# Expert blocks of 64 token slots in place of 96, with room for 23 further blocks, and the down bias added ahead of the expert loop

## The reference, cut to what matters

```python
logits = (h @ w_router + b_router).astype(jnp.float32)
top_val, top_idx = lax.top_k(logits, TOP_K)            # 4 of 32
gate = jax.nn.softmax(top_val, axis=-1)
...
def expert_block(args):
    tok, e = args
    gu = h[tok] @ w_gate_up[e] + b_gate_up[e]
    return clamped_swiglu(gu) @ w_down[e] + b_down[e]
...
y = y * slot_w[:, None].astype(y.dtype)
return jnp.zeros_like(h).at[slot_tok].add(y)
```

## Time and profile before

| what | value |
|---|---|
| median of three runs | 1408.8 us |
| the profiled execution, whole | 1410.75 us |
| its span, first to last instruction | 1408.9 us |
| around the span | 1.85 us |
| granted TensorE clock over the span | 0.959 of full speed |
| TensorE busy | 1294.7 us, 92% of the span |
| moved by DMA | 497.97 MB, mean 353 GB/s |

### The profile page before, as it was taken

How to read it: one execution, slowest core, us unless ns; L and a number is a source line. 1 busy time by engine, 2 the same in 40 slices (tenths; PEclk the granted TensorE clock), 3 DMA queues, 4 the chain that set the end, 5 groups by cost and what they waited for, 6 DMA issues and landing times.

```text
span 1408.9 us, 40022 instructions
## 1 busy us (share of the span) xinstructions
PE 1294.7 (92%) x17444; PEld 820.4 (58%) x17444; DVE 474.1 (34%) x917; ACT 260.2 (18%) x552; POOL 202.1 (14%) x279
## 2 busy tenths in 40 slices
PE   4898999972999999999999999999999999999980
PEld 1796666851566666556666666556666666566640
DVE  0112555655222323322322323322323323322326
ACT  1123444122111111111111111111111111111102
POOL 2205220711100000011000000011000000011003
PEclk9898999985999999999999999999999999999995
DMA  9955586216999999999999999999999999999916
GB/s 332 380 180 173 185 276 213 72 60 253 350 422 423 423 422 423 423 422 423 422 423 423 422 423 420 422 422 422 423 422 423 423 419 422 423 422 423 418 43 223
DMA packets 91214, 497.97 MB, mean 353 GB/s; under 512 B 11972, under 2 KB 15060, under 8 KB 41184
## 3 DMA queue, kind: packets, MB, share of 16 engines
q1 hardware_dynamic: 69552, 437.98, 76.0%
q0 software_dynamic: 13232, 38.78, 7.7%
q10 hardware_dynamic: 8400, 20.82, 4.0%
HBM read 475.20 MB, written 23.25 MB: 354 GB/s over the span
## 4 chain that ended last, share of the span: by engine, by line
PE 72%; DMA 2%; DVE 1%; issue 1%; POOL 0%; ACT 0%; DVEq 0%; ACTq 0%; POOLq 0%
PE ps L1752 47%; PE ps L1765 16%; PE ps L1770 7%; DMA h_rows<-h_parts 2%; PE ps L1739 1%; DVE y_got L1352 1%; PE ps L1720 0%; DMA y_got<-y_rows,y_row_idx 0%; DVE y_got L1357 0%; DMA y_rows<-y_blk 0%; DMA x_slots<-h_rows,slot_tok 0%; POOL y_got L654 0%; DVE x L1364 0%; DVE x L1358 0%; POOL x_slots L640 0%
## 5 line engine op out<-in xcount | busy, mean ns | idle before, releaser
L1752 PE MATMUL ps<-ring,xT 128*32 128x256 f32 x9216 | 511.0, 380 | 9.0 <-DVE xT L1291 9.0
L1752 PEld LDWEIGHTS ps<-ring,xT 128*32 128x32 f32 x9216 | 346.1, 110 | 176.1 <-issue 12.2
L1765 PE MATMUL ps<-y_got,aT 128*32 128x512 f32 x2048 | 279.3, 593 | 0.0
L1305 DVE TENSOR_TENSOR raw<-ps,bias_row 128x768 f32<-128x768 f32 x64 | 61.3, 958 | 474.2 <-PE ps L1752 474.2
L1752 PE MATMUL ps<-y_got,xT 128*32 128x256 f32 x3072 | 176.9, 379 | 0.0
L1770 PE MATMUL ps<-y_got,aT 128*32 128x512 f32 x1024 | 168.6, 592 | 0.0
L1765 PEld LDWEIGHTS ps<-y_got,aT 128*32 128x32 f32 x2048 | 99.0, 109 | 96.4 <-issue 52.4
L1752 PEld LDWEIGHTS ps<-y_got,xT 128*32 128x32 f32 x3072 | 116.0, 110 | 52.4
L891 ACT ACTIVATE sig<-glu 128x384 f32<-128x384 f32 x64 | 33.5, 523 | 574.4 <-DVE glu L1308 574.4
L630 POOL COPY cur_idx<-slot_tok 128x3 int32 x32 | 5.9, 185 | 842.5 <-DVE xT L1291 842.5
L634 POOL DMA_INDIRECT x_slots<-h_rows,cur_idx x96 | 92.0, 958 | 46.4 <-POOL cur_idx L630 24.1
(11 more groups left out here) (276 smaller groups left out, 993.6 us busy)
## 6 DMA issues: line engine op xcount, KB each, us to landing
ring<-in_moe_w SPq DMA_DIRECT2D x192, 1024.0 KB, 8.1
y_got<-in_moe_w SPq DMA_DIRECT2D x192, 1024.0 KB, 7.7
ring<-in_ada_w SPq DMA_DIRECT2D x24, 1024.0 KB, 7.2
y_rows<-y_blk ACTq DMA_DIRECT2D x32, 384.0 KB, 6.7
ring<-in_in_w SPq DMA_DIRECT2D x6, 960.0 KB, 13.6
y_rows<-qabs POOLq DMA_DIRECT2D x15, 384.0 KB, 13.0
latT<-in_cache_lat_t POOLq DMA_DIRECT2D x8, 512.0 KB, 3.9
lat<-in_cache_lat POOLq DMA_DIRECT2D x8, 512.0 KB, 4.0
```

Source lines behind the costliest of these rows:

```text
L1305: nc.vector.tensor_tensor(raw[:, f], gate_up(f), bias_row[:, f, :].unsqueeze(1).to_broadcast([P, NSUB, 2 * P]), ALU.add).then_inc(S["gu_em ...
L1752: ins = nc.tensor.matmul(out.rearrange("p (a n) -> p a n", a=8), xT[:, g, 2 * j + k, :], w[:, k, :, q, :], start=(j == 0 and k == 0), stop ...
L1765: nc.tensor.matmul(main[q * SUB:(q + 1) * SUB, :], a_of(kt0 + k, g), w[:, k, c, :], start=False, stop=(last and k == 1))
```

## The change

A block gets two groups of 32 slots, 64 in all (`NSUB`, `CAP`). The table of blocks grows from 48 columns to 56, for up to 23 further blocks. A unit of gate and up is then 16 products and a unit of down 8; the third group's products, the half-width copies and the two VectorE sums are gone. The down bias leaves the loop: ahead of it TensorE multiplies each token's four gates by the experts' down biases (`gates_T` by `b_down`, L1800 of the new file), and VectorE scales that by the residual gate and adds it to x (`add_base`). The residual gate is formed ahead of the loop instead of behind it. In the routing VectorE has 29 instructions where it had 56 between the logits and the table's operands; a prefix scan takes the place of five shift-and-add steps, one row number for each choice takes the place of block and position, and the table's operands are bfloat16. SP issues units 6 to 8 only when `h_rows` has been stored, and units 9 to 11 only when the first gather has landed.

In the rows below a number such as 32x256 is the written shape, "x15" counts repeats, and the square bracket names the semaphores that an instruction waits for.

The diff, cut to its core:

```diff
-NSUB = 3
+NSUB = 2
 ROW = D // 4
-MAIN = 64
-CAP = 96
+CAP = NSUB * SUB
 NOVF = NT * P * TOPK // (CAP + 1)
 NBLK = NE + NOVF + 1
...
-        emptied(sp, "logit", NT - 1)
+        emptied(sp, "logit")
+        sp.wait_ge(S["h_stored"], 16 * NT)
         for j in range(SLOTS, MOE_UNITS):
+            if j == SLOTS + 3:
+                sp.wait_ge(S["gathered"], 16 * NSUB)
             nc.sync.dma_start(moe_place(j), moe_w[0, j]).then_inc(moe_sem(j), 16)
...
+        a.wait_ge(S["gates_exped"], NT)
+        a.wait_ge(S["logits_exp"], 1)
+        for t in range(NT):
+            for k in range(TOPK):
+                ins = nc.scalar.activation(hot_gate[:, t * TOPK + k, :], route_hot[:, t * TOPK + k, :], ACT.Copy,
+                                           scale=gate_w[:, t, k:k + 1])
+            ins.then_inc(S["hot_scaled"], 1)
+        a.wait_ge(S["bias_ready"], 1)
+        for k in range(2):
+            for f in range(2):
+                filled(a, "gf", k, f)
+                empty(("gf", k, f), gate_f[:, k, f * 512:(f + 1) * 512], bank("gf", k, f))
+        filled(a, "GT")
+        empty(("GT",), gates_T[:, :], bank("GT")[0:NT * NE, 0:P])
...
-            nc.scalar.copy(half_y[:, :], ps[MAIN:P, 7, :]).then_inc(S["y_half"], 1)
             a.wait_ge(S["y_stored"], i * 16 + 16)
-            nc.scalar.copy(y_blk[0:MAIN, 0:512], ps[0:MAIN, 6, :])
-            nc.scalar.copy(y_blk[0:MAIN, 512:D], ps[MAIN:P, 6, :]).then_inc(S["y_copied"], 1)
+            nc.scalar.copy(y_blk[:, 0:512], ps[0:CAP, 6, :])
+            nc.scalar.copy(y_blk[:, 512:D], ps[CAP:P, 6, :]).then_inc(S["y_copied"], 1)
...
-        d = 1
-        while d < NE:
-            nc.vector.tensor_copy(alt[:, 0:d], cum[:, 0:d])
-            step(nc.vector.tensor_tensor(alt[:, d:NE], cum[:, d:NE], cum[:, 0:NE - d], ALU.add))
-            cum, alt, d = alt, cum, 2 * d
...
+        step(nc.vector.tensor_tensor_scan(cum, before[:, 1, 0:NE], n_own, 0.0, ALU.mult, ALU.add))
...
-        for fsrc, dst in ((pos, pos_of), (blk, blk_of)):
-            for t in range(NT):
-                last = nc.vector.tensor_tensor(prod[:, t * TOPK:(t + 1) * TOPK, :], hot[:, t * TOPK:(t + 1) * TOPK, :],
-                                               fsrc[:, t:t + 1, :].to_broadcast([P, TOPK, NE]), ALU.mult)
-            step(last)
-            step(nc.vector.tensor_reduce(dst, prod, AX, ALU.add))
...
+        step(nc.vector.tensor_tensor(prod.rearrange("p (t k) e -> p t k e", t=NT), hot.rearrange("p (t k) e -> p t k e", t=NT),
+                                     rank.unsqueeze(2).to_broadcast([P, NT, TOPK, NE]), ALU.mult))
+        step(nc.vector.tensor_reduce(y_row, prod, AX, ALU.add))
...
+        def add_base(n):
+
+            t, b0 = BASE[n]
+            v.wait_ge(S["base_filled"], n + 1)
+            nc.vector.scalar_tensor_tensor(squares, ps[:, b0:b0 + 2, :].rearrange("p a b -> p (a b)"), stat[:, 50 + t:51 + t],
+                                           gate_f[:, t // 2, :], ALU.mult, ALU.mult).then_inc(S["base_emptied"], 1)
+            v.wait_ge(S["base_emptied"], n + 1)
+            step(nc.vector.tensor_tensor(x[:, t, :], x[:, t, :], squares, ALU.add))
+
+        emptied(v, "gf", 1, 1)
+        add_base(0)
         turn_x(0)
-        v.sem_inc(S["y_summed"], 1)
+        add_base(1)
+        add_base(2)
...
-            v.wait_ge(S["y_half"], i + 1)
-            v.wait_ge(S["y_stored"], i * 16 + 16)
-            nc.vector.tensor_tensor(y_blk[MAIN:CAP, 0:512], ps[0:SUB, 7, :], half_y[0:SUB, :], ALU.add)
-            nc.vector.tensor_tensor(y_blk[MAIN:CAP, 512:D], ps[SUB:MAIN, 7, :], half_y[SUB:MAIN, :], ALU.add).then_inc(
-                S["y_summed"], 1)
...
+        for k in range(2):
+            spread([("gf", k, f) for f in range(2)], (10, 11), k)
...
+        out = open_job("GT")
+        pe.wait_ge(S["hot_scaled"], NT)
+        for k in range(TOPK):
+            for t in range(NT):
+                ins = nc.tensor.matmul(out[t * NE:(t + 1) * NE, 0:P], hot_gate[:, t * TOPK + k, :], ident[:, :], start=(k == 0),
+                                       stop=(k == TOPK - 1))
+        close(ins)
...
-                        nc.tensor.matmul(main[q * SUB:(q + 1) * SUB, :], a_of(kt0 + k, g),
-                                         w[:, k, c, :], start=False, stop=(last and k == 1))
-            for k in range(2):
-                for c in range(2):
-                    q = 2 * k + c
-                    ins = nc.tensor.matmul(extra[q * SUB:(q + 1) * SUB, :], a_of(kt0 + k, 2), w[:, k, c, :],
-                                           start=(first and k != 0), stop=last)
+                        ins = nc.tensor.matmul(main[q * SUB:(q + 1) * SUB, :], a_of(kt0 + k, g),
+                                               w[:, k, c, :], start=(first and k == 0), stop=(last and k == 1))
...
+            pe.wait_ge(S["base_emptied"], 1)
             for n in range(8):
+                if n == 4:
+                    pe.wait_ge(S["base_emptied"], 2)
...
+        for c in range(2):
+            for t, b0 in BASE:
+                r = slice(t * NE, (t + 1) * NE)
+                ins = nc.tensor.matmul(ps[:, b0 + c, :], gates_T[r, :], b_down[r, c * 512:(c + 1) * 512], start=True, stop=True)
+                if c == 1:
+                    ins.then_inc(S["base_filled"], 1)
...
-        pe.wait_ge(S["gu_emptied"], (n_ovf + NE) * 2 + 2)
-        pe.wait_ge(S["bias_copied"], n_ovf + (NE + 1))
-        for part in range(3):
-            for k in range(2):
-                for f in range(2):
-                    r = slice(64 + 32 * f, 96 + 32 * f)
-                    ins = nc.tensor.matmul(ps[:, 2 * k + f, :], kind_sel[r, k, :], mod_parts[r, 1, part, :],
-                                           start=(part == 0), stop=(part == 2))
-        ins.then_inc(S["gates_filled"], 1)
```

More of the change, by code:

```diff
@@ L142, in psum_jobs @@
     late += [(("fT", t, g), "a") for t in range(NT) for g in range(2)]
-    late += [(("logitT",), "a")] + [(("logit", t), "v") for t in range(NT)]
-    late += [(("rank", t), "v") for t in range(NT)] + [(("count",), "v"), (("table",), "v")]
+    late += [(("logitT",), "a")] + [(("logit",), "v"), (("rank",), "v")]
+    late += [(("gf", k, f), "a") for k in range(2) for f in range(2)] + [(("table",), "v"), (("GT",), "a")]
     return early, late
@@ L1243, in _ @@
[L1243 to L1251 removed]
+        nc.vector.tensor_reduce(chosen[:, :, :], hot.rearrange("p (t k) e -> p t e k", t=NT), AX, ALU.max).then_inc(
+            S["logits_exp"], 1)
@@ L1690, in _ @@
         emptied(pe, "logitT")
+        out = open_job("logit")
         for t in range(NT):
[L1692 to L1693 removed]
+            ins = nc.tensor.matmul(out[:, t * NE:(t + 1) * NE], ksT[:, t * P:(t + 1) * P], fold[:, :], start=True, stop=True)
+        close(ins)
         pe.wait_ge(S["logits_exp"], 1)
[L1695 to L1703 removed]
+        out = open_job("rank")
+        for t in range(NT + 1):
+            for s in range(min(t + 1, NT)):
+                ins = nc.tensor.matmul(out[:, t * NE:(t + 1) * NE], before[:, 1 if s < t else 0, :], chosen[:, s, :],
+                                       start=(s == 0), stop=(s == min(t, NT - 1)))
         close(ins)
+        for k in range(2):
+            spread([("gf", k, f) for f in range(2)], (10, 11), k)
         pe.wait_ge(S["placed"], 1)
@@ L1714, in _ @@
         pe.wait_ge(S["bias_ready"], 1)
-        def bias_main(main, cols, open_group=True):
-            for c in range(2):
-                for g in range(2):
-                    q = 2 * c + g
-                    nc.tensor.matmul(main[q * SUB:(q + 1) * SUB, :], sel_e[:, :], bias_parts[:, cols[c]:cols[c] + 512],
-                                     start=open_group, stop=not open_group)
-        def bias_extra(extra, cols, half, open_group=True):
-            for c in range(2):
-                q = 2 * half + c
-                ins = nc.tensor.matmul(extra[q * SUB:(q + 1) * SUB, :], sel_e[:, :], bias_parts[:, cols[c]:cols[c] + 512],
-                                       start=open_group, stop=not open_group)
-            return ins
         bias_gu = bias_parts[:, 0:2 * D].rearrange("p (f q n) -> p f q n", f=2, q=4)
@@ L1735, in bias_gate_up @@
             pe.wait_ge(S["sel_ready"], i + 1)
-            pe.wait_ge(S["gu_emptied"], i * 2 + 2)
-            for f in range(2):
-                for q in range(4):
-                    ins = nc.tensor.matmul(bias_tile(f)[q * SUB:(q + 1) * SUB, :], sel_e[:, :], bias_gu[:, f, q, :],
-                                           start=True, stop=True)
+            if not isinstance(i, int):
+                pe.wait_ge(S["bias_copied"], i)
+            for q in range(4):
+                ins = nc.tensor.matmul(ps[q * SUB:(q + 1) * SUB, 4, :].rearrange("p (f n) -> p f n", f=2), sel_e[:, :],
+                                       bias_gu[:, :, q, :], start=True, stop=True)
             ins.then_inc(S["bias_tiled"], 1)
@@ L1754, in gate_up_products, with down_products @@
```

(2 more changed lines are left out.)

198 lines of the change are left out of this document (92 added, 106 removed).

## The result

The changed kernel takes 1457.0 us (median of 4 runs, 1455.3 to 1457.3), the kernel before 1408.6 beside it: a ratio of 1.0342, interval 1.0324 to 1.036. The forecast was 1450, the range 1435 to 1471. From one profiled execution to the other it is 1457.13 against 1410.75, 46.4 us more where the sum said 41.1; the span is 1455.3.

The account below looks back on a forecast made before the run. TensorE at 31.67 us a block bounds the kernel, DMA almost equally; afterwards DMA does. Start -5.4, loop +47.7 and end -1.2 make +41.1 on 1410.75, or 1451.9; less 1.95, predicted 1450 us, range 1435 to 1471.

Parts of the forecast that it names:

- Two limits that all but coincide: Expert loop of the kernel before: TensorE sets the pace at 31.67 us a block, DMA at nearly the same.
- DMA takes over at 31.04 us: Expert loop after the change: DMA becomes the limit at 31.04 us a block, and TensorE waits 10 us in each.
- Three further blocks: Second loop: three experts exceed 64 slots, giving 35 blocks in all, each further one loading its expert's 12 MiB again.
- The lead-in: Loop's beginning: 6.5 us until block 0's last load lands, besides 34 blocks at DMA's pace and 2.1 us behind.
- The loop's start: Ahead of the loop: shorter routing and early stores start it at 343.6 instead of 349.01, 5.4 us earlier.
- that term: Ahead of the loop: four down-bias products on TensorE at half clock, bounds 2 to 7 us, 4.5 taken.
- The end: Behind the loop: the half copy and two sums go from before the last store, saving 1.2 us; the rest stays.
- The last subtraction: Whole kernel: 1.95 us that the profiled execution lay over the median, turning 1451.9 into the predicted 1450.
- A: Loop: DMA had room beyond 422 GB/s; a gain from 29.84 us a block (439 GB/s); chance 4%.
- B: Loop: DMA gets slower when it alone sets the pace; 1474 us at 413 GB/s; chance 8% for over 1470.
- D: Second loop: no further blocks run, 31 blocks at DMA pace follow block 0, 1357 us; chance 2%.
- C: Loop: TensorE's waits drop its clock to 0.50 for good, 42.2 us a block, 1870 us; chance 2%.

Follow-up runs that it names:

- Run 7: The kernel before with half of the loop's expert products left out, all weights still loaded: 1385.2 us, ratio 0.983.
- run 3: The changed kernel with each load from block 1 on bringing only half of every row, all products made: 1121.2 us, ratio 0.7954.
- run 12: The changed kernel with 192 unused bytes a partition ahead of the row buffers (`x_slots` and those behind it) alone: 1452.1 us, ratio 1.0303.
- run 1: The changed kernel without its further blocks, slots above 64 of the three fuller experts left out: 1363.5 us, ratio 0.9676.
- run 6: The changed kernel without SP's two new waits, so block 0's last six loads start as early as before: 1460.6 us, ratio 1.0372.
- run 2: The changed kernel with half of the loop's expert products left out, all weights still loaded: 1454.5 us, ratio 1.0325.
- run 5: The changed kernel with four loads standing in the queue instead of eleven, from block 2 on: 1459.5 us, ratio 1.0355.
- the lighter kernel: 96-slot kernel with the change's other edits; for 29 experts no third-group products and fewer rows gathered and stored: 1377.0 us, ratio 0.9769.
- run 11: The 96-slot kernel with fewer products and row bytes for 29 experts, plus 480 unused bytes a partition ahead of `x_slots`: 1370.1 us, ratio 0.9728.
- runs 8 and 9: 96 slots with the change's other edits, third-group products only for three fuller experts: 1383.5 us; then also fewer row bytes for the other 29: 1377.0 us.

## Why the prediction was right, step by step

**Two limits that all but coincide: right, shown.** Run 7 puts the transfers at 31.63 us a block beside TensorE's 31.67. (In the earlier trace rows the full stretch begins later than was read: the share is full from the eleventh slice, and the rate is 418 to 423 GB/s from the twelfth.)

**TensorE falls to 21.1 us a block: right.** 20.90 in run 3.

**DMA takes over at 31.04 us: right in kind, short in size.** It measured 31.17, and 34 blocks make 4.3 us of it (1059.8 against 1055.5). The term took the bytes of a block at the rate of the rows of before, and so took for granted that a byte costs the same in the changed layout. It did not: with the buffers from `x_slots` on back at their old offsets a block took 31.02 (run 12). No row of before could show this. The 358 GB/s for a core in the Trainium skill, "DMA: Bandwidth & Descriptors", section "Specifications", are again passed by 421 over 850 us, and its 435 are not reached.

**Three further blocks: right.** 35 stores, and 93.5 us for the three (run 1).

**The lead-in: 2.7 us short.** The loop's 1071.1 less 34 x 31.17 leave 11.3, not 8.6. The windows hold most of it: 6 us at 329 GB/s and 30 us at 408 are 1.3 and 0.9 us of lost rate against 421; what the last 0.5 us are is open.

**The loop's start: -7.1 instead of -5.4.** The last routing step was done at 333.8, not 335, and `add_base` began 3.9 us after the first base product instead of 4.5. (The bounds of 2 to 7 us for that term do not follow from 0.6 to 2.4 us a pair, which make 1.2 to 4.8 for two pairs; the 4.5 taken lies in both.) Runs with the same code ahead of the loop started it between 340.9 and 343.4, so the 1.7 us lie within their spread. That SP's new waits let the stores land early is shown by run 6, 5.0 us of the start.

**The end: -1.2, as forecast, but in part by luck.** From the last product to the last store it is 1.58 us instead of 2.40, so 0.8 of the 1.2 forecast there; the other 0.4 lie between that store and the first gather (3.76 us instead of 4.13), a stretch that the prediction let stay.

**The last subtraction.** 1.95 us were taken off because the profiled execution of before lay over its median; the changed kernel's (1457.13) lay at its own (1457.01). With the 5.3 us of the terms that is the 7 us between 1450 and 1457.

**The rivals.** A fell: with half of the products left out the transfers still ran at 421 GB/s and 31.15 us a block (26 in 809.78 us, run 2), far from the 29.84 it needed. B fell as put: 421, no lower for a queue of eleven (run 5). D fell with the 35 stores. C did not happen: TensorE waited at nearly every unit, and the clock stayed at 1.00 from 480 to 1330 us. In run 2, where longer waits stood between half the products, it was granted at 0.50 and 0.84 in the two stretches shown, and the time stayed; what the low clock would cost with all products was not tried. The Trainium skill, "TensorE: Matmul & The Clock Gate", section "HAM oscillation — how this bites in real kernels", tells of a kernel that fell back to the low clock in each of its waits for DMA, which were longer than the work between them. The trace of the changed kernel, with waits of 0.4 to 1.2 us after 1.9 us of work, shows no fall; that of run 2 does, off the path that sets the end. Two of the prediction's sums do not come out: C's time would be near 1863, not 1870, and a start 8 us later together with 417 GB/s gives 1471, not 1465. Neither decides anything here.

## What to carry to other kernels

Where two limits coincide, a cut in one of them buys only what the other leaves: a third less TensorE work was worth at most 8.5 us in 1392 here, while each further block cost 31 us of weights read again. Cut the work that is not shared (products, rows) for the light cases by a branch, and keep what is read once (weights) read once. When a kernel is bound by transfers, look at where its buffers lie before trusting a rate from another layout to better than half a per cent.

## What the runs showed of the hardware

The offset in SBUF of a group of buffers, two of which hold the small rows, changed the pace of all transfers: at 0 within 512 bytes, 422 to 423 GB/s and 31.02 us a block; at 320, 421 and 31.17; in the lighter kernel at 32, 419 and 31.47, and at 0, 421 and 31.30 (14 light blocks alone, 31.38 and 31.20). The rows are 4% of the bytes. What in the chip does it, no run here shows.

Loads with 4 KB in each row instead of 8 moved fewer bytes for the same share: from 500 to 1000 us of run 3, 150.55 MB at 85.1%, 354 GB/s for a full share; the changed kernel's 322.83 MB in 800 us at 97.1% are 416. TensorE set the pace in run 3, so this is no limit that a run reached.

```profile
q1 hardware_dynamic: 41345, 150.55, 85.1%
```

In run 11 two blocks began 5.0 and 5.8 us after the block before them with no wait that the profile names. Each was the second block after TensorE's branch had changed sides (to the fuller experts and back), and runs 8 and 9 have the same two gaps. The queue of instruction loads moved 11 packets from 620 to 780 us of run 11, one of them within each gap, and none from 480 to 620 or from 780 to 1230; that these loads cause the gaps is likely and not shown. The slack of 10 us in the lighter blocks took the second one up. That gap, and the queue from 620 to 780 us:

```profile
735.51 4.79 PE L1804 MATMUL ps<-ring,xT 128*32 128x256 f32 x44 [5.83 <-issue]
...
q8 instruction: 11, 0.18, 0.5%
```
